# Where a matmul's operands begin: split activations and weights laid 16 bytes further apart

## The chip, the cores and the metric

The kernel runs on one core of one Trainium2 chip. The metric is the device time of one launch in microseconds (us), the median of several runs; less is better.

## The reference

One decoder block on x of 1 x 1024 x 1024 float32: a half-step SwiGLU FFN, a mixer, a second half-step FFN, and a final norm. Each part is preceded by an RMS norm, which is shifted, scaled and gated by vectors made from c.

```python
def swiglu(h, w1, w3, w2):
    return (jax.nn.silu(h @ w1) * (h @ w3)) @ w2
...
        h = modulate(rmsnorm(x, g_ffn1[l]), sh1, sc1)
        x = x + 0.5 * gt1[:, None, :] * swiglu(h, ffn1_w1[l], ffn1_w3[l], ffn1_w2[l])
        h = modulate(rmsnorm(x, g_mix[l]), sh2, sc2)
        x = x + gt2[:, None, :] * hybrid_mixer(
            h, w_in[l], lambda_q1[l], lambda_k1[l], lambda_q2[l], lambda_k2[l],
            subln_g[l], conv_w[l], conv_norm_g[l], w_out[l], cos, sin, lambda_init)
        h = modulate(rmsnorm(x, g_ffn2[l]), sh3, sc3)
        x = x + 0.5 * gt3[:, None, :] * swiglu(h, ffn2_w1[l], ffn2_w3[l], ffn2_w2[l])
```

The FFNs have D_MODEL 1024 and D_FF 2816. The mixer has 4 heads of differential attention and a short gated convolution.

## The kernel before

Activations lie transposed, 128 features by 512 positions to a tile; `X` holds the residual stream. All wide products are made from float32r parts: an operand a is split in hi and lo, and a product a b is three matmuls, hi hi, hi lo and lo hi, each 128 x 128 weights over a moving operand of 128 x 512. ACT writes the hi part (a copy to float32r) and DVE the lo part (a subtraction).

In an FFN the up part (`up`, `ph` 0 and 1 for the two FFNs) uses Strassen's scheme over 2 x 2 halves: seven products, `j` = 0 to 6. For product `j` the moving operand is `Bh[j]`, `Bl[j]`, four tiles of 128 x 512 each. A first group (`plain_group`) makes plain products with `Bh` and `Bl` of 0, 5, "B12" and 3. Then each `u` from 2 to 21 makes the seven jobs in the order of `j`. One job is 12 matmuls: four blocks k, and for each the three

```python
mm_open(PS[:, bank, :], Wh[:, t % SLOTS, w], Bh[j][:, k, :], fresh and k == 0, False)
mm_open(PS[:, bank, :], Wh[:, t % SLOTS, w], Bl[j][:, k, :], False, False)
made = mm_open(PS[:, bank, :], Wl[:, t % SLOTS, w], Bh[j][:, k, :], False, last and k == KH - 1)
```

The second argument is the weights, the third the moving operand; `t` counts jobs, so that job `t` finds its weights in slot `t % 8` of the ring `Wh`, `Wl`. The down part (`down`, `down_tile`) uses the same scheme with jobs `m`; here both operands come through the ring: the weights `Wh[:, 4 + m % 4, ...]` and `Wl` of the same slot, the moving operand `Wh[:, m % 4, :]` and `Wl` of that slot. `prep_hi`, `down_hi` (ACT) and `prep_lo`, `down_lo` (DVE) fill the ring. Every matmul is preceded by its own load of weights (engine PEld in the profile).

The mixer's projections have moving operands `Hh`, `Hl` and weights `Mh`, `Ml`; the projection to V has them the other way round; the last heads' output projection moves `Gh`, `Gl` or `G2` over `Wo`.

All tiles are placed by hand, with `place(..., like=address)`, in bytes from the start of a partition. `base` is 16512, K is 1024. The order on each engine is written out by hand; semaphores tie the engines together.

Of the kernel before, what the change touches and what calls it, by code (L numbers as in the profile page):

```python
# [6 lines left out]
F32R = mybir.dt.float32r  # L7
# [4 lines left out]
P = 128  # L12
# [3 lines left out]
KH = KT // 2  # L16
HALF = 512
# [55 lines left out]

PAIRS = 2 * NG
SLOTS = 8
AHEAD = 5
AHEAD_B = 3
N_UP = 8 + 7 * (PAIRS - 2)
# [72 lines left out]
def program(nc, up_w, down_w, units, ada, x_t, cols_d, lam_d, rope_d, square_d, out_t):  # L151
    ctx = ExitStack()
    with ctx:
# [3 lines left out]
        def place(name, shape, dtype=F32, like=None):  # L157

            size = 4
            for n in shape[1:]:  # L160
                size *= n
            offset = at[0] if like is None else like
            if like is None:
                at[0] += (size + 31) // 32 * 32
            return nc.alloc_sbuf_tensor_at(name, shape, dtype, offset=offset), offset

        K = 1024
        base = at[0]
        x_at = base + 88 * K + 64
        slot_at, raw_at, t_at, z_at, tmp_at = (x_at + n * K for n in (32, 64, 80, 96, 108))  # L170
        at[0] = tmp_at + 8 * K

        X, _ = place("X", [P, NH, KT, HALF], like=x_at)
# [3 lines left out]
        Bh, Bl = {}, {}  # L177
        for _j, _h, _l in ((0, base, base + 8 * K), (1, base + 16 * K, base + 24 * K), (2, base + 32 * K, base + 40 * K),
                           (3, base + 48 * K, base + 56 * K), (5, base + 64 * K, base + 72 * K),
                           (4, x_at + 24 * K, x_at + 16 * K), (6, x_at + 8 * K, x_at),  # L180
                           ("B12", z_at + 4 * K, tmp_at)):
            Bh[_j], _ = place(f"Bh{_j}", [P, KH, HALF], F32R, like=_h)
            Bl[_j], _ = place(f"Bl{_j}", [P, KH, HALF], F32R, like=_l)
        Sums, _ = place("Sums", [P, 4, HALF], like=base + 80 * K)
        Wh, _ = place("Wh", [P, SLOTS, HALF], F32R, like=slot_at)
        Wl, _ = place("Wl", [P, SLOTS, HALF], F32R, like=slot_at + 16 * K)
        Raw, _ = place("Raw", [P, 4, 2, HALF], like=raw_at)
        T, _ = place("T", [P, 8, HALF], like=t_at)
        Ada, _ = place("Ada", [P, 2, D], like=z_at)
        AdaSum, _ = place("AdaSum", [P, D], like=z_at + 8 * K)  # L190
        W2s, _ = place("W2s", [P, 4, HALF], like=tmp_at)
# [3 lines left out]
        RawB, _ = place("RawB", [P, 8, HALF], like=raw_at)  # L195

        AdaFirst, _ = place("AdaFirst", [P, KT, D], like=base)
        AdaSecond, _ = place("AdaSecond", [P, KT, D], like=base + 32 * K)
        AdaSum0, _ = place("AdaSum0", [P, D], like=t_at)
        AdaRow, _ = place("AdaRow", [P, D], like=t_at + 4 * K)  # L200
        Lam4, _ = place("Lam4", [P, 4, DH], like=t_at + 8 * K)
        LamP, _ = place("LamP", [P, 2, DH], like=t_at + 9 * K)


        Mh, _ = place("Mh", [P, RING, S], F32R, like=base)
        qk_at = base + 12 * K
        QK, _ = place("QK", [P, 2, S + 8], like=qk_at)
        CU, _ = place("CU", [P, S + 2], like=qk_at)
        CT, _ = place("CT", [P, S], like=qk_at + 4 * (S + 8))
        o_at = qk_at + 8 * (S + 8)  # L210
        O, _ = place("O", [P, QB, P], like=o_at)
        Mr, _ = place("Mr", [P, RING, S], like=o_at + 4 * K)
        h0_at = o_at + 16 * K
# [3 lines left out]
        Ml, _ = place("Ml", [P, RING, S], F32R, like=h0_at + 32 * K)  # L217

        Wo, _ = place("Wo", [P, 2, 2, S], F32R, like=h0_at)
        Rope, _ = place("Rope", [P, 2, S], like=h0_at + 44 * K)  # L220
        assert h0_at + 52 * K == x_at
        V, _ = place("V", [P, QB, HEADS * P], like=raw_at)
        Gh, _ = place("Gh", [P, GF, S], F32R, like=t_at)
        Gl, _ = place("Gl", [P, GF, S], F32R, like=t_at + 8 * K)
        NextQ, _ = place("NextQ", [P, S], like=t_at + 4 * K)
        NextK, _ = place("NextK", [P, S], like=t_at + 12 * K)

        G2, _ = place("G2", [P, 2, S + 8], F32R, like=qk_at)
        PR, _ = place("PR", [P, 3, S], like=z_at)
        SqSum, _ = place("SqSum", [P, NH, HALF], like=z_at)  # L230
        Sq, _ = place("Sq", [P, 2, HALF], like=z_at + 4 * K)
        Spread, _ = place("Spread", [P, NH, HALF], like=z_at + 8 * K)
        TmpA, _ = place("TmpA", [P, 2, HALF], like=tmp_at)
        TmpG, _ = place("TmpG", [P, 2, HALF], like=tmp_at + 4 * K)
        DT, _ = place("DT", [P, S], like=tmp_at + 4 * K)
        Out, _ = place("Out", [P, NH, KT, HALF], like=h0_at)

        Square, _ = place("Square", [P, 2, P])
        Cols, _ = place("Cols", [P, NCOLS])
        Mod, _ = place("Mod", [P, SECTIONS * KT])  # L240
        Scale, _ = place("Scale", [P, 4, KT])
        Gate, _ = place("Gate", [P, 3, KT])
        CAct, _ = place("CAct", [P, KT])
        Ones, _ = place("Ones", [P, 1])
        Mean, _ = place("Mean", [P, 1])
        MeanG, _ = place("MeanG", [P, 2])
        EpsC, _ = place("EpsC", [P, 2])
        Root, _ = place("Root", [P, 8])
        Inv, _ = place("Inv", [P, 8])
        LamS, _ = place("LamS", [P, 8])  # L250
        SubG, _ = place("SubG", [P, 1])
        NMax, _ = place("NMax", [P, 2])
        Sum, _ = place("Sum", [P, 2])
        RSum, _ = place("RSum", [P, QB, 2])
        Ratio, _ = place("Ratio", [P, 1])
        Junk, _ = place("Junk", [P, P])
        SqO, _ = place("SqO", [P, QB])
# [17 lines left out]
        def blk(b):  # L275
            return slice(b * P, (b + 1) * P)
# [123 lines left out]
        def _(sp):  # L400
# [11 lines left out]
            def spill(ph, g, q):  # L412
                sp.wait_ge(mul_done, silu_no(ph, g, q))
                sp.dma_start(g_dram[ph][g, q], T[:, 4 + q, :]).then_inc(spilled[q], 16)
# [25 lines left out]
            def block_of(ph):  # L440
# [4 lines left out]
                for t in range(8, N_UP):  # L445
                    u, j = 2 + (t - 8) // 7, (t - 8) % 7
                    u2, j2 = 2 + (t - 8 + AHEAD) // 7, (t - 8 + AHEAD) % 7
                    if j2 == 6 and u2 + 2 < PAIRS:
                        load_up(ph, u2 + 2)
                    up, jp = 2 + (t - 9) // 7, (t - 9) % 7  # L450
                    if t > 8 and up % 2 and jp >= 3:
                        spill(ph, up // 2, Q_OF_J[jp])
                    if t == N_UP - AHEAD:
                        for m in range(8):
# [145 lines left out]
        def _(act):  # L600
            def prep_hi(ph, o):

                slot = o % SLOTS
                if o < 8:
# [8 lines left out]
                else:  # L613
# [3 lines left out]
                    else:  # L617
                        act.wait_ge(prod, N_FFN * ph + max(o - SLOTS + 1, 8))
                    if j in (0, 5, 6):
# [61 lines left out]
            def t_hi(ph, n, j):  # L681
                h, k = {1: (0, 0), 2: (0, 0), 4: (1, 0), 6: (0, 0)}[j]
                for a in (0, 2):
                    act.wait_ge(t_sum, 8 * ph + 2 * n + a // 2 + 1)
                    nc.scalar.activation(Bh[j][:, a:a + 2, :], X[:, h, k + a:k + a + 2, :], ACT.Copy).then_inc(bt_hi, 1)

            def up(ph):
# [22 lines left out]
                for t in range(8, N_UP):  # L710
                    if t == 10:
                        t_hi(ph, 3, 6)
                    if t + AHEAD < N_UP:
                        prep_hi(ph, t + AHEAD)
                    elif t + AHEAD_B >= N_UP:
# [278 lines left out]
        def _(dve):  # L994
            def prep_lo(ph, o):

                slot = o % SLOTS
                if o < 8:
# [110 lines left out]
            def t_lo(ph, n, j):  # L1109
                h, k = {1: (0, 0), 2: (0, 0), 4: (1, 0), 6: (0, 0)}[j]  # L1110
                for a in (0, 2):
                    dve.wait_ge(bt_hi, 8 * ph + 2 * n + a // 2 + 1)
                    nc.vector.tensor_tensor(Bl[j][:, a:a + 2, :], X[:, h, k + a:k + a + 2, :],
                                            Bh[j][:, a:a + 2, :].bitcast(F32), ALU.subtract).then_inc(b_lo, 1)

            def up(ph):
# [37 lines left out]
                for t in range(8, N_UP):  # L1154
                    if t == 10:
                        t_add(ph, 3, 6)
                        t_lo(ph, 3, 6)
                    if t + AHEAD < N_UP:
                        prep_lo(ph, t + AHEAD)
                    elif t + AHEAD_B >= N_UP:  # L1160
# [369 lines left out]
        def _(pe):  # L1530
# [3 lines left out]
            def mm_open(out, lhs, rhs, first, last):  # L1534

                return nc.tensor.matmul(out, lhs, rhs, start=first, stop=last, skip_group_check=True)  # L1536
# [69 lines left out]
            def up(ph):  # L1606
                plain_group(ph)
                for t in range(8, N_UP):
# [8 lines left out]
                    for k in range(KH):  # L1617
                        w = blk(k)
                        mm_open(PS[:, bank, :], Wh[:, t % SLOTS, w], Bh[j][:, k, :], fresh and k == 0, False)
                        mm_open(PS[:, bank, :], Wh[:, t % SLOTS, w], Bl[j][:, k, :], False, False)  # L1620
# [450 lines left out]
```

## Time and profile before

| | |
|---|---|
| median of 3 runs | 1904.79 us (1899.98 to 1904.81) |
| span of the profiled execution | 1904.1 us |
| TensorE busy | 1834.6 us, 96% |
| DVE busy | 1262.7 us, 66% |
| ACT busy | 773.6 us, 41% |
| POOL busy | 269.8 us, 14% |

The profile gives one execution's span, from its first to its last instruction; the median of the runs is 0.7 us longer. Busy time of TensorE is counted from start to modelled end of matmuls that overlap, so how fast it gets through them is read from the starts.

### The profile page before, as it was taken

How to read it: one execution, taken by the hardware profiler on the slowest of the kernel's cores; microseconds unless marked ns; L12 is line 12 of the kernel's file. 1: busy time of each engine (PE TensorE's matmuls, PEld its weight loads, DVE VectorE, ACT ScalarE, POOL GpSimd, SP SyncE). 2: the span in 40 equal slices, each digit the busy share in tenths (PEclk: the TensorE clock that was granted, in tenths of full speed). 3: DMA queues.
4: the chain of work that ended last, by engine and by line, in shares of the span. 5: the costliest groups of instructions: out<-in, count | busy, mean ns of one | idle time of the engine just before them, and what ended most of it. 6: DMA issues, size and time to landing. Idle time of an engine off the chain costs nothing.

```text
span 1904.1 us, 22925 instructions
## 1 busy us (share of the span) xinstructions
PE 1834.6 (96%) x8248; PEld 1466.7 (77%) x8248; DVE 1262.7 (66%) x1952; ACT 773.6 (41%) x1392; POOL 269.8 (14%) x411
## 2 busy tenths in 40 slices
PE   5999999999999999999999999899999999999997
PEld 2878888888788877888876666687888888878885
DVE  5887777767486776444326668787667666577767
ACT  5643333333344555111125555563333333344445
POOL 2011211211210000000303330101111211112000
PEclk9999999999999999999999999999999999999998
DMA  8165565664775321111211110325454544477432
GB/s 316 64 230 198 198 218 192 225 210 168 265 216 155 95 64 74 45 45 45 67 33 45 45 34 1 140 83 197 160 189 170 204 156 168 158 261 217 128 99 89
DMA packets 100528, 269.76 MB, mean 142 GB/s; under 512 B 13120, under 2 KB 13504, under 8 KB 100288
## 3 DMA queue, kind: packets, MB, share of 16 engines
q1 hardware_dynamic: 62608, 146.30, 22.6%
q0 software_dynamic: 34304, 117.46, 18.2%
q10 hardware_dynamic: 3504, 4.53, 1.0%
q8 instruction: 66, 1.08, 0.2%
q14 instruction: 46, 0.38, 0.1%
HBM read 209.53 MB, written 54.53 MB: 139 GB/s over the span
## 4 chain that ended last, share of the span: by engine, by line
PE 84%; DVE 8%; ACT 4%; issue 2%; DMA 1%; ACTq 1%; POOL 1%; DVEq 0%; POOLq 0%
PE PS L1536 60%; PE PS L1532 24%; DMA AdaFirst<-ada 1%; PE PS L1956 1%; ACTq L877 1%; DVE X L1107 1%; DVE NMax L1447 1%; DVE Wl L1006 1%; DVE Ml L1246 0%; ACT X L676 0%; DVE SqSum L1312 0%; DVE TmpA L1330 0%; DVE X L1343 0%; DVE Wl L1041 0%; ACT PR L899 0%
## 5 line engine op out<-in xcount | busy, mean ns | idle before, releaser
L1536 PE MATMUL PS<-Bh,Wh 128*128 128x512 f32 x1120 | 441.4, 394 | 3.7 <-ACT T L659 3.7
L1536 PE MATMUL PS<-Bl,Wh 128*128 128x512 f32 x1120 | 440.6, 393 | 0.0
L1536 PE MATMUL PS<-Bh,Wl 128*128 128x512 f32 x1120 | 439.9, 393 | 0.0
L1536 PEld LDWEIGHTS PS<-Bh,Wh 128*128 128x128 f32 x1120 | 209.8, 187 | 55.7 <-issue 3.7
L1536 PEld LDWEIGHTS PS<-Bh,Wl 128*128 128x128 f32 x1120 | 209.8, 187 | 49.9
L1536 PEld LDWEIGHTS PS<-Bl,Wh 128*128 128x128 f32 x1120 | 209.8, 187 | 49.1
L1536 PE MATMUL PS<-Wh 128*128 128x512 f32 x616 | 240.3, 390 | 3.4 <-DVE Wl L1041 1.7
L1536 PE MATMUL PS<-Wh,Wl 128*128 128x512 f32 x616 | 239.7, 389 | 0.0
L1536 PE MATMUL PS<-Wl,Wh 128*128 128x512 f32 x616 | 239.7, 389 | 0.0
L1038 DVE TENSOR_TENSOR Wl<-RawB,Wh 128x512 fp32r<-128x512 f32 x154 | 106.6, 692 | 136.5 <-ACT Wh L634 135.3
L634 ACT ACTIVATE Wh<-RawB 128x512 fp32r<-128x512 f32 x154 | 97.3, 632 | 230.0 <-PE PS L1536 230.0
L659 ACT ACTIVATE T<-PS 128x512 f32<-128x512 f32 x120 | 71.7, 597 | 257.3 <-PE PS L1536 257.3
L1006 DVE TENSOR_TENSOR Wl<-Sums,Wh 128x512 fp32r<-128x512 f32 x160 | 110.3, 689 | 88.2 <-ACT Wh L624 88.1
L1536 PEld LDWEIGHTS PS<-Wh 128*128 128x128 f32 x616 | 115.6, 188 | 28.6 <-DVE T L1072 2.5
L1006 DVE TENSOR_TENSOR Wl<-Raw,Wh 128x512 fp32r<-128x512 f32 x136 | 94.6, 700 | 61.9 <-ACT Wh L624 61.4
L1536 PEld LDWEIGHTS PS<-Wl,Wh 128*128 128x128 f32 x616 | 115.7, 188 | 23.9
L1536 PEld LDWEIGHTS PS<-Wh,Wl 128*128 128x128 f32 x616 | 115.6, 188 | 23.9
L1532 PE MATMUL PS<-Hh,Mh 128*128 128x512 f32 x320 | 131.6, 411 | 2.1 <-DVE Hl L1336 1.3
L624 ACT ACTIVATE Wh<-Sums 128x512 fp32r<-128x512 f32 x160 | 98.4, 623 | 80.1 <-DVE Sums L1024 52.6
L1532 PE MATMUL PS<-Hl,Mh 128*128 128x512 f32 x320 | 127.4, 398 | 0.0
L1532 PE MATMUL PS<-Hh,Ml 128*128 128x512 f32 x320 | 126.8, 396 | 0.0
L1062 DVE TENSOR_TENSOR T<-T,PS 128x512 f32<-128x512 f32 x120 | 82.3, 686 | 47.2 <-PE PS L1536 45.2
(193 smaller groups left out, 2869.7 us busy)
## 6 DMA issues: line engine op xcount, KB each, us to landing
Raw<-up_w SPq DMA_DIRECT2D x86, 512.0 KB, 5.5
Ada<-ada POOLq DMA_DIRECT2D x72, 512.0 KB, 4.2
g_dram<-T SPq DMA_DIRECT2D x88, 256.0 KB, 2.1
W2s<-down_w POOLq DMA_DIRECT2D x88, 256.0 KB, 4.4
s_dram<-W2s POOLq DMA_DIRECT2D x88, 256.0 KB, 2.6
GQ<-g_dram POOLq DMA_DIRECT2D x88, 256.0 KB, 3.3
RawB<-s_dram SPq DMA_DIRECT2D x88, 256.0 KB, 2.8
RawB<-down_w SPq DMA_DIRECT2D x66, 256.0 KB, 2.7
```

What stands on the lines that cost most here:

```text
L624: nc.scalar.activation(Wh[:, slot, :], src, ACT.Copy).then_inc(w_hi, 1)
L634: nc.scalar.activation(Wh[:, 4 + m % 4, :], RawB[:, m % 8, :], ACT.Copy).then_inc(w_hi, 1)
L659: nc.scalar.activation(T[:, 4 * w + q, :], PS[:, x + (j == 1), :], ACT.Copy).then_inc(acopy, 1)
L877: act.dma_start(to[a:a + 32, :], TmpA[a ^ 32:(a ^ 32) + 32, slot, :]).then_inc(shifted[j % 2], 16)
L1006: nc.vector.tensor_tensor(Wl[:, slot, :], src, Wh[:, slot, :].bitcast(F32), ALU.subtract).then_inc(w_lo, 1)
L1038: nc.vector.tensor_tensor(Wl[:, 4 + m % 4, :], RawB[:, m % 8, :], Wh[:, 4 + m % 4, :].bitcast(F32), ALU.subtract).then_inc(w_lo, 1)
L1062: nc.vector.tensor_tensor(T[:, 4 * w + q, :], T[:, 4 * w + q, :], PS[:, x + (j != 4), :], ALU.add)\
L1107: nc.vector.tensor_tensor(out, left, right, ALU.subtract).then_inc(t_sum, 1)
L1447: nc.vector.tensor_reduce(NMax[:, c:c + 1], scores(c, 0, i + 1), AX.X, ALU.max, negate=True)\
L1532: return nc.tensor.matmul(out, lhs, rhs, start=first, stop=last)
L1536: return nc.tensor.matmul(out, lhs, rhs, start=first, stop=last, skip_group_check=True)
L1956: made = nc.tensor.transpose(PS[:, 4 + r, blk(b % 4)], PR[:, 2, blk(b)], ident)
```

## The change

Three kinds of addresses are moved; nothing else is touched. Each of the eight slots of `Wh` and `Wl` becomes 16 bytes wider, so that slot n begins 16 n bytes later than it did. The tiles `Bh[j]`, `Bl[j]` of `j` = 0, 1, 2, 3, 5 are moved up by 0, 32, 64, 96, 128 bytes, and of each `Bl` another 16. What lies behind them is moved up to make room, by multiples of 128 bytes but for `Sums` (160). The instructions of each engine, their order and their waits are the same as before.

```diff
@@ -73,6 +73,7 @@
 
 PAIRS = 2 * NG
 SLOTS = 8
+SKEW = 16
 AHEAD = 5
 AHEAD_B = 3
 N_UP = 8 + 7 * (PAIRS - 2)
@@ -166,8 +167,9 @@
 
         K = 1024
         base = at[0]
-        x_at = base + 88 * K + 64
-        slot_at, raw_at, t_at, z_at, tmp_at = (x_at + n * K for n in (32, 64, 80, 96, 108))
+        x_at = base + 88 * K + 192
+        slot_at = x_at + 32 * K
+        raw_at, t_at, z_at, tmp_at = (slot_at + n * K + 2 * SLOTS * SKEW for n in (32, 48, 64, 76))
         at[0] = tmp_at + 8 * K
 
         X, _ = place("X", [P, NH, KT, HALF], like=x_at)
@@ -179,11 +181,16 @@
                            (3, base + 48 * K, base + 56 * K), (5, base + 64 * K, base + 72 * K),
                            (4, x_at + 24 * K, x_at + 16 * K), (6, x_at + 8 * K, x_at),
                            ("B12", z_at + 4 * K, tmp_at)):
-            Bh[_j], _ = place(f"Bh{_j}", [P, KH, HALF], F32R, like=_h)
-            Bl[_j], _ = place(f"Bl{_j}", [P, KH, HALF], F32R, like=_l)
-        Sums, _ = place("Sums", [P, 4, HALF], like=base + 80 * K)
-        Wh, _ = place("Wh", [P, SLOTS, HALF], F32R, like=slot_at)
-        Wl, _ = place("Wl", [P, SLOTS, HALF], F32R, like=slot_at + 16 * K)
+            n = (0, 1, 2, 3, 5).index(_j) * 2 * SKEW if _j in (0, 1, 2, 3, 5) else 0
+            lead = SKEW // 4 if _j in (0, 1, 2, 3, 5) else 0
+            Bh[_j], _ = place(f"Bh{_j}", [P, KH, HALF], F32R, like=_h + n)
+            whole, _ = place(f"Bl{_j}", [P, lead + KH * HALF], F32R, like=_l + n)
+            Bl[_j] = whole[:, lead:lead + KH * HALF].rearrange("p (k s) -> p k s", k=KH)
+        Sums, _ = place("Sums", [P, 4, HALF], like=base + 80 * K + 10 * SKEW)
+        wide = HALF + SKEW // 4
+        Wh, _ = place("Wh", [P, SLOTS, wide], F32R, like=slot_at)
+        Wl, _ = place("Wl", [P, SLOTS, wide], F32R, like=slot_at + 16 * K + SLOTS * SKEW)
+        Wh, Wl = Wh[:, :, 0:HALF], Wl[:, :, 0:HALF]
         Raw, _ = place("Raw", [P, 4, 2, HALF], like=raw_at)
         T, _ = place("T", [P, 8, HALF], like=t_at)
         Ada, _ = place("Ada", [P, 2, D], like=z_at)
@@ -218,7 +225,7 @@
 
         Wo, _ = place("Wo", [P, 2, 2, S], F32R, like=h0_at)
         Rope, _ = place("Rope", [P, 2, S], like=h0_at + 44 * K)
-        assert h0_at + 52 * K == x_at
+        assert h0_at + 52 * K <= x_at
         V, _ = place("V", [P, QB, HEADS * P], like=raw_at)
         Gh, _ = place("Gh", [P, GF, S], F32R, like=t_at)
         Gl, _ = place("Gl", [P, GF, S], F32R, like=t_at + 8 * K)
```

## Rows read from the trace of the kernel before

**Rows 1.** The page: span; busy us of each engine, share, instructions.

```profile
span 1904.1 us, 22925 instructions
...
PE 1834.6 (96%) x8248; PEld 1466.7 (77%) x8248; DVE 1262.7 (66%) x1952; ACT 773.6 (41%) x1392; POOL 269.8 (14%) x411
```

**Rows 2.** The page: the chain of work that ended last, by engine and by line.

```profile
PE 84%; DVE 8%; ACT 4%; issue 2%; DMA 1%; ACTq 1%; POOL 1%; DVEq 0%; POOLq 0%
PE PS L1536 60%; PE PS L1532 24%; DMA AdaFirst<-ada 1%; PE PS L1956 1%; ACTq L877 1%; DVE X L1107 1%; DVE NMax L1447 1%; DVE Wl L1006 1%; DVE Ml L1246 0%; ACT X L676 0%; DVE SqSum L1312 0%; DVE TmpA L1330 0%; DVE X L1343 0%; DVE Wl L1041 0%
```

**Rows 3.** TensorE's groups by shape: count, busy us, mean ns, idle before; one per kind.

```profile
L1536 PE MATMUL PS<-Bh,Wh 128*128 128x512 f32 x1120 | 441.4, 394 | 3.7 <-ACT T L659 3.7
...
L1536 PE MATMUL PS<-Wh 128*128 128x512 f32 x616 | 240.3, 390 | 3.4 <-DVE Wl L1041 1.7 <-DVE T L1072 1.6
...
L1532 PE MATMUL PS<-Bh,Wh 128*128 128x512 f32 x96 | 40.3, 419 | 5.8 <-DVE Bl L1097 5.8
...
L1532 PE MATMUL PS<-BlB,Wh 128*128 128x512 f32 x32 | 12.5, 390 | 0.0
```

**Rows 4.** Windows, engine busy us (instructions): unit of seven jobs, jobs, down, mixer.

```profile
core 0: us, PE busy (x) PEld busy (x) DVE busy (x) ACT busy (x) POOL busy (x), PEclk, DMA share, GB/s
247.05:266.51 19.46, 19.46 (x85) 15.68 (x84) 16.85 (x24) 5.14 (x9) 4.83 (x9) 1.00 0.66 232
263.71:266.51 2.80, 2.80 (x13) 2.24 (x12) 1.14 (x2) 1.12 (x2) 2.14 (x4) 1.00 0.91 345
266.51:269.25 2.74, 2.74 (x13) 2.25 (x12) 1.92 (x3) 1.15 (x2) 0.54 (x1) 1.00 0.91 286
269.25:272.05 2.80, 2.80 (x13) 2.25 (x12) 2.63 (x4) 1.15 (x2) 0.42 (x1) 1.00 0.23 83
503.16:519.48 16.32, 16.32 (x73) 13.52 (x72) 8.93 (x14) 6.92 (x12) 3.23 (x6) 1.00 1.02 376
827.49:835.73 8.24, 8.24 (x37) 6.76 (x36) 2.68 (x4) 0.00 (x0) 0.00 (x0) 1.00 0.00 1
836.42:839.17 2.75, 2.75 (x14) 2.25 (x12) 0.69 (x1) 0.64 (x1) 0.00 (x0) 1.00 0.00 0
952.44:958.07 5.63, 5.63 (x25) 4.51 (x24) 0.00 (x0) 0.00 (x0) 0.00 (x0) 1.00 0.26 93
1199.49:1202.29 2.80, 2.80 (x13) 2.25 (x12) 0.81 (x2) 1.89 (x4) 0.00 (x0) 1.00 0.84 275
```

**Rows 5.** Timeline of TensorE: start us, us; the job of `j` = 4.

```profile
266.51 0.39 PE L1536 MATMUL PS<-Bh,Wh 128*128 128x512 f32 x1
266.74 0.40 PE L1536 MATMUL PS<-Bl,Wh 128*128 128x512 f32 x1
266.98 0.39 PE L1536 MATMUL PS<-Bh,Wl 128*128 128x512 f32 x1
267.20 0.40 PE L1536 MATMUL PS<-Bh,Wh 128*128 128x512 f32 x1
267.44 0.39 PE L1536 MATMUL PS<-Bl,Wh 128*128 128x512 f32 x1
267.67 0.39 PE L1536 MATMUL PS<-Bh,Wl 128*128 128x512 f32 x1
267.89 0.39 PE L1536 MATMUL PS<-Bh,Wh 128*128 128x512 f32 x1
268.12 0.39 PE L1536 MATMUL PS<-Bl,Wh 128*128 128x512 f32 x1
```

**Rows 6.** DVE's subtractions on line 1006, by input.

```profile
L1006 DVE TENSOR_TENSOR Wl<-Sums,Wh 128x512 fp32r<-128x512 f32 x160 | 110.3, 689 | 88.2 <-ACT Wh L624 88.1
...
L1006 DVE TENSOR_TENSOR Wl<-Raw,Wh 128x512 fp32r<-128x512 f32 x136 | 94.6, 700 | 61.9 <-ACT Wh L624 61.4
```

## The prediction

> **What bounds the kernel now.** I read the page first: TensorE is busy for 96% of the span, DVE for 66%, ACT for 41% [rows 1], and the chain of work that ended last lies on TensorE for 84%, 60% of the span on line 1536 alone [rows 2]. Line 1536 issues the products of both FFNs; as long as they follow each other without a gap, each nanosecond more or less between two of them is one in the result. So I read next how many there are, by tile, and then, in windows that begin and end on a job of the program, how far apart two of them start. Their durations (390 to 419 ns, [rows 3]) are of no use for that, since matmuls overlap; the distance from start to start (the pitch) is.
>
> The pitch is not one number [rows 4]. In the windows the count of weight loads is the count of matmuls, and TensorE is busy throughout. A job of `j` = 3 (from 263.71) takes 2.80 us for 12 matmuls, 233.3 ns each; the job of `j` = 4 behind it 2.74 us, 228.3 ns; that of `j` = 5 again 2.80 us. In the down part (from 503.16) 72 matmuls take 16.32 us, 226.7 ns. The granted clock is 1.00 in all. DMA doesn't make the difference: the two 2.80 us jobs have a DMA share of 0.91 and 0.23. The slots of the weights are the same in both.
>
> What differs is where the operands begin. I call an address modulo 128 its phase: `base` is 16512, so phase 0, and `x_at` and all behind it phase 64. Before the change `Wh` and `Wl` have phase 64, `Bh` and `Bl` of `j` = 0, 1, 2, 3, 5 phase 0, those of 4, 6 and "B12" phase 64. Call the moving operand's phase less the weights' the distance. Distance 64 (opposite) goes with 233.3 ns, distance 0 with 226.7. The start of the job of `j` = 4 shows how the fast pitch is reached [rows 5]: starts 0.23, 0.24, 0.22, 0.24, 0.23, 0.22, 0.23 us apart. The change of distance takes six or seven matmuls to settle, which is why such a job stands at 228.3 and not at 226.7.
>
> Three further places tell more [rows 4]. In the projections (from 827.49, 36 matmuls in 8.24 us, 228.9 ns) the moving operand always has phase 64, the weights 0, 0, 64 in turn. In the values' projection (from 952.44, 24 in 5.63 us, 234.5 ns) the weights keep 64 and the moving operand goes 0, 0, 64. In the output projection of the last heads (from 1199.49, 12 in 2.80 us, 233.3 ns) the weights keep 64 and the moving operand goes 0, 32, 0. So the weights' phase counts too, not the moving operand's alone; and distance 96 (32 less 64) is as dear as distance 64.
>
> **The change, part by part.** No instruction, wait or transfer is added, removed or moved; only addresses change. After it, slot n of `Wh` and of `Wl` has phase 64 + 16n; `Bh` of `j` = 0, 1, 2, 3, 5 has 0, 32, 64, 96, 0 and `Bl` 16 more; `j` = 4, 6 and "B12" keep 64. `X`, the DMAs' targets and everything of the mixer keep their phases (`Sums` goes to 32).
>
> ACT writes and DVE reads and writes at new phases. I cost that at nothing: the same subtraction takes 689 ns with an input at phase 0 and 700 ns with all at 64 [rows 6]. What hides it otherwise is TensorE's own 19.46 us in a unit of seven jobs, in which DVE is busy for 16.85 and ACT for 5.14 [rows 4]; DVE's 24 instructions there would each have to grow by 0.1 us before anything waits.
>
> *The down part.* A job `m` reads its weights in slot 4 + m % 4 and its moving operand in slot m % 4. Before, both have phase 64: distance 0. After, they are 64 apart for every m: distance 64 throughout. The matmuls there are three groups of 616, 1848 [rows 3]. Bounds: no loss, 0; the pitch of the other rows at constant distance 64, 233.3 - 226.7 = 6.67 ns, x 1848 = 12.3 us. Between them lies the projections' row, with moving 64 over weights 0 in two of three: (228.9 - 226.7) x 1848 = 4.1 us. I take 12.3, since there, as in the up jobs of `j` = 3, the distance stays for the whole job and doesn't alternate.
>
> *The up part.* Seven jobs go round eight slots, so each `j` meets all eight distances about equally often. Matmuls on line 1536: 3 x 1120 = 3360, of which 5/7 = 2400 at distance 64 now and 960 at distance 0; the plain group adds 3 x 96 = 288 at 64 and 3 x 32 = 96 at 0 [rows 3]. So 2688 stand at 233.3, 960 at 228.3, 96 at 226.7. What a distance costs is known for 0 (228.3 with the settling), 64 and 96 (233.3 each); five are not shown. Bounds for these: 228.3 and 233.3. I take the middle, 230.8: of the five, 16 and 112 lie beside the cheap 0, 48 and 80 beside the dear 64, and 32 between. Mean: (228.3 + 2 x 233.3 + 5 x 230.8) / 8 = 231.1 ns. The shift of 16 between `Bh` and `Bl` I cost at nothing: the row with 0, 32, 0 stands at 233.3, as without the alternation.
> - 2688 x (231.1 - 233.3) = -5.9 us
> - 960 x (231.1 - 228.3) = +2.7 us
> - 96 x (231.1 - 226.7) = +0.4 us
>
> With the five unknown at 228.3 the mean is 229.6 and the three terms are -9.9 + 1.2 + 0.3 = -8.4 us; at 233.3 it is 232.7, and they are -1.6 + 4.2 + 0.6 = +3.2 us.
>
> Sum: -5.9 + 2.7 + 0.4 + 12.3 = +9.5 us on the profiled execution's span of 1904.1 us, 1913.6. The median of the three runs is 1904.8, 0.7 above that span, so 1914.3.
>
> A rule speaks against any effect. The rows just read show two pitches, 233.3 and 226.7 ns, at the same clock. The Trainium skill, "TensorE: Matmul & The Clock Gate" (Part 2, Step-by-step), has it that TensorE reads moving operand and weights through two independent ports, so that loading the next weights takes no read bandwidth from the running matmul; by that the sum is 0. "SBUF — State Buffer" (Who interferes with whom) says likewise that TensorE waits for no one. The trace doesn't agree: its pitch follows the pair of phases.
>
> **The rivals.**
> - *Gain and loss cancel.* The five unknown distances are all cheap (228.3): -8.4 + 12.3 = +3.9 us, 1908.7, inside what can't be told from no change. For it speaks that the change of distance settles in six matmuls; against it that 96 is dear.
> - *Faster.* The opposite distance is dear only with the weights ahead: moving 64 over weights 0 would be cheap. For it speaks the projections' 228.9. Then the down part loses nothing, and with cheap neighbours the sum is -8.4 us, 1896.4. It decides for faster once the down part loses under about 2.7 us, 1.5 ns a matmul. Its far end is every product at 226.7: 2688 x 6.67 + 960 x 1.67 = 19.5 us less, 1885.
> - *Dearer than either pitch.* Changing phases cost by themselves, as in the values' projection (234.5), and all products come there: 2688 x 1.2 + 960 x 6.2 + 96 x 7.8 + 1848 x 7.8 = 24.4 us, 1929. Against it: 0, 32, 0 costs nothing.
> - *No effect of phases.* The two pitches come from something else that goes with the tiles, such as how high in memory they lie (`Bh` of 4 and 6 lie behind `x_at`, the others ahead of it). Then 1904.8. Against it: the projections have the same pitch with `Hh0` ahead of `x_at` (228.9) and with `Hh1` behind it (12 in 2.75 us, 229) [rows 4].
>
> **How the numbers follow.** Forecast 0.45, cancelling 0.19, faster 0.22, dearer still 0.10, no effect 0.04. 0.3% (5.7 us) is about what a measurement of this kernel can tell from no change. Faster 0.22; same 0.19 + 0.04 = 0.23; slower 0.45 + 0.10 = 0.55. The forecast's own range is 1911 (down part at 12.3, up part at -6) to 1920 (12.3 + 3.2). For 8 in 10 it takes in the faster rival down to 1894 and goes up to 1922, leaving out most of "dearer still" and the far end of "faster".
>
> **What would show it.** The down part's windows: 233.3 instead of 226.7 ns between starts; if 226.7 stays there, the main term falls. The up jobs: pitches that differ by slot, 227 to 233, with a mean near 231, and the jobs of `j` = 4 and 6 no longer faster than the rest. Projections, values and attention: unchanged. DVE's and ACT's durations within 2% of before. Wrong would be the whole if a distance not shown before has a pitch under 226 or over 240.

## The result, and the profile after

The median of five runs is 1909.49 us, against 1903.05 before: the ratio is 1.0034, with a 95% interval of 1.0018 to 1.0051. The kernel became 6.4 us slower; the forecast was 9.5 slower. The time lies in the wide range of 1894 to 1922 us, and 1.5 us below the forecast's own range of 1911 to 1920. The profiled execution has a span of 1911.3 us, 7.2 above that of [rows 1].

The page after: the span, the engines and the chain. Against [rows 1, 2] TensorE is busy 8.8 us longer, DVE and ACT as long as before, and TensorE's share of the chain went from 84 to 86%.

```profile
span 1911.3 us, 22925 instructions
...
PE 1843.4 (96%) x8248; PEld 1468.7 (77%) x8248; DVE 1261.7 (66%) x1952; ACT 774.1 (41%) x1392; POOL 270.4 (14%) x411
...
PE 86%; DVE 7%; ACT 3%; issue 1%; DMA 1%; ACTq 1%; POOL 1%; DVEq 0%; POOLq 0%
```

Where the 7.2 us lie is read from windows over the stages. First those of the kernel before: up and down part of the first FFN, the mixer, up and down part of the second. The columns are as in [rows 4].

```profile
43.68:496.49 452.81, 449.46 (x1977) 363.85 (x1977) 336.72 (x483) 173.63 (x291) 78.86 (x147) 0.99 0.54 188
496.49:711.69 215.20, 212.17 (x942) 175.03 (x941) 153.66 (x247) 102.72 (x175) 17.74 (x33) 1.00 0.51 156
711.69:1230.17 518.48, 489.36 (x2353) 380.57 (x2351) 280.67 (x467) 194.32 (x419) 76.40 (x55) 0.98 0.16 52
1230.17:1674.00 443.83, 443.43 (x1937) 358.77 (x1937) 306.97 (x450) 174.81 (x294) 67.23 (x124) 1.00 0.47 164
1674.00:1889.68 215.68, 212.01 (x941) 174.87 (x940) 155.44 (x248) 101.46 (x174) 17.75 (x33) 1.00 0.51 158
```

The same stages after the change:

```profile
44.81:497.60 452.79, 449.52 (x1977) 365.00 (x1977) 336.69 (x483) 173.84 (x291) 78.88 (x147) 0.99 0.53 188
497.60:716.60 219.00, 216.49 (x941) 175.01 (x940) 153.73 (x246) 102.81 (x175) 17.73 (x33) 1.00 0.50 153
716.60:1234.39 517.79, 489.46 (x2353) 380.62 (x2351) 279.50 (x467) 194.25 (x419) 76.95 (x55) 0.98 0.16 52
1234.39:1678.29 443.90, 443.52 (x1936) 360.01 (x1937) 307.00 (x450) 175.14 (x294) 67.27 (x124) 1.00 0.47 165
1678.29:1897.96 219.67, 216.44 (x941) 174.90 (x940) 155.50 (x248) 101.41 (x174) 17.75 (x33) 1.00 0.50 155
```

Both up parts take as long as before (452.81 and 452.79 us, 443.83 and 443.90). The down parts take 3.80 and 3.99 us more. The mixer takes 0.7 less; what lies ahead of the first stage takes 1.1 more and what lies behind the last 1.1 less.

Windows after the change, which answer to [rows 4]: an up job of `j` = 4 and the one of `j` = 5; 12 jobs of the down part; the projections with `Hh0` and with `Hh1`; the values' projection; the last heads' output projection.

```profile
267.55:270.33 2.78, 2.78 (x13) 2.25 (x12) 1.95 (x3) 1.15 (x2) 0.54 (x1) 1.00 0.70 267
270.33:273.14 2.81, 2.81 (x14) 2.26 (x13) 2.60 (x4) 1.15 (x2) 0.43 (x1) 1.00 0.42 122
509.75:543.09 33.34, 33.34 (x146) 27.04 (x145) 24.00 (x38) 13.85 (x24) 6.45 (x12) 1.00 0.76 247
829.36:837.60 8.24, 8.24 (x37) 6.76 (x36) 2.68 (x4) 0.00 (x0) 0.00 (x0) 1.00 0.00 1
838.29:841.07 2.78, 2.78 (x13) 2.25 (x12) 0.69 (x1) 0.63 (x1) 0.00 (x0) 1.00 0.00 0
954.73:960.29 5.56, 5.56 (x25) 4.51 (x24) 0.00 (x0) 0.00 (x0) 0.00 (x0) 1.00 0.25 94
1202.71:1205.48 2.77, 2.77 (x13) 2.25 (x12) 0.78 (x2) 1.89 (x4) 0.00 (x0) 1.00 0.78 290
```

In the down part 144 matmuls take 33.34 us, 231.5 ns each, against 226.7. The up job of `j` = 4 takes 2.78 us (231.3) where it took 2.74, that of `j` = 5 2.81 for 12 (2.80 before). And the mixer did move, though modulo 128 none of its tiles had: with `Hh0` 36 matmuls still take 8.24 us, but with `Hh1` 12 take 2.78 instead of 2.75; the values' projection went from 5.63 to 5.56, the output projection from 2.80 to 2.77.

DVE's subtractions, which answer to [rows 6], are no dearer at the new phases:

```profile
L1013 DVE TENSOR_TENSOR Wl<-Sums,Wh 128x512 fp32r<-128x512 f32 x160 | 110.3, 689 | 87.3 <-ACT Wh L631 87.2
...
L1013 DVE TENSOR_TENSOR Wl<-Raw,Wh 128x512 fp32r<-128x512 f32 x136 | 93.9, 695 | 63.4 <-ACT Wh L631 63.3
```

### The profile page after: what moved, and what is told of

Read it like the earlier page. It is cut to its first block, busy times and chain, and to the rows that moved or that the text cites. A ratio compares the mean times of both kernels' runs of the same rounds, so it can differ in the third digit from the quotient of the medians.

```text
span 1911.3 us, 22925 instructions
## 1 busy us (share of the span) xinstructions
PE 1843.4 (96%) x8248; PEld 1468.7 (77%) x8248; DVE 1261.7 (66%) x1952; ACT 774.1 (41%) x1392; POOL 270.4 (14%) x411
## 4 chain that ended last, share of the span: by engine, by line
PE 86%; DVE 7%; ACT 3%; issue 1%; DMA 1%; ACTq 1%; POOL 1%; DVEq 0%; POOLq 0%
PE PS L1543 60%; PE PS L1539 25%; PE PS L1963 1%; DMA AdaFirst<-ada 1%; ACTq L884 1%; DVE NMax L1454 1%; DVE Ml L1253 1%; DVE SqSum L1319 0%; DVE TmpA L1337 0%; DVE Wl L1048 0%; ACT PR L906 0%; DVE Wl L1013 0%; DMA TmpA<-TmpA 0%; DVE CT L1419 0%; DVE Wl L1045 0%
```

## The experiments

Throughout, the distance is the moving operand's address less the weights'. Three runs were timed several times (`same64`, `mixer_too`, `odd16`); the others have one time each and are told by their traces. The diffs are shortened: remarks in brackets are not code, and lines that only make room for the moved tiles are left out.

### One phase for all operands of the FFNs: same64

```diff
-            Bh[_j], _ = place(f"Bh{_j}", [P, KH, HALF], F32R, like=_h)
-            Bl[_j], _ = place(f"Bl{_j}", [P, KH, HALF], F32R, like=_l)
+            n = {0: 64, 1: 64, 2: 64, 3: 64, 5: 64}.get(_j, 0)
+            (both placed at like=_h + n, like=_l + n)
-        Sums, _ = place("Sums", [P, 4, HALF], like=base + 80 * K)
+        Sums, _ = place("Sums", [P, 4, HALF], like=base + 80 * K + 64)
```

> The kernel before with the five low pairs of Bh and Bl moved up by 64 bytes, so that every FFN operand begins at 64 modulo 128: distance 0 everywhere. If the pitch follows the distance between moving operand and weights (theory of the prediction), all seven kinds of up job stand at 226.7 ns and the run is 2688 x 6.67 + 960 x 1.67 = 19.5 us faster, about 1884 us. If it followed something else that goes with the tiles (how high in memory they lie, their order), the five stay at 233.3 ns and the time at 1903 us.

Measured: 1886.27 us, ratio to the kernel before 0.9911 (0.9895 to 0.9928). Its stages, up, down, mixer, up:

```profile
44.55:489.10 444.55, 441.93 (x1976) 365.31 (x1977) 336.39 (x483) 173.61 (x291) 79.19 (x147) 0.99 0.55 192
489.10:704.23 215.13, 212.07 (x941) 175.03 (x940) 153.62 (x247) 102.83 (x175) 17.79 (x33) 1.00 0.50 156
704.23:1223.80 519.57, 490.41 (x2354) 381.08 (x2352) 279.76 (x467) 194.84 (x419) 77.13 (x55) 0.98 0.16 52
1223.80:1659.23 435.43, 434.11 (x1936) 359.52 (x1937) 306.99 (x450) 174.64 (x294) 67.48 (x124) 1.00 0.47 168
```

The up parts lose 8.26 and 8.40 us, the down part none; that is 16.7 of the 19.5 expected. Of the 2.8 us that are missing, 1.9 lie where two starts are over 300 ns apart: beyond a usual pitch such places hold 0.9 us more than before in the first up part and 1.0 in the second, nearly all in `u` = 2, the first unit of seven jobs. In the second this is idle time (443.83 - 443.43 = 0.40 us before, 435.43 - 434.11 = 1.32 now). In the first, idle time fell by 0.7, but behind a wait of 2.33 us for ACT the granted clock was 0.55 from 101.07 to 104.84 us (the lower level, 1.2 GHz, for most of it), and matmuls started 427 ns apart. The median job of each `j` stands at 226.7 ns from its first matmul on; where the distance doesn't change there is nothing to settle. The tiles moved by 64 bytes and kept their order and height in memory, so height is not what sets the pitch. Whether an operand's own place modulo 256 counts beside the distance is asked of `moved96` and `odd16` below.

### The distances one by one: near, far, wide

```diff
-        x_at = base + 88 * K + 64
+        x_at = base + 88 * K + 64 + 512
...
+            n = {0: 16, 1: 32, 2: 48, 3: 64, 5: 80}.get(_j, 0)      (near)
+            n = {0: 96, 1: 112, 2: 128, 3: 160, 5: 192}.get(_j, 0)  (far)
+            n = {0: 224, 1: 256, 2: 288, 3: 320, 5: 448}.get(_j, 0) (wide)
```

> The kernel before with Bh and Bl of j = 0, 1, 2, 3, 5 moved up by 16, 32, 48, 64, 80 bytes (all behind them by 512): constant distances of -48, -32, -16, 0, 16 bytes between moving operand and weights, the down part as before. By the theory of the prediction, with distances modulo 128, the second half of the jobs stands at 233.3 ns for j = 1 (96), 226.7 for j = 3 (0), and between them for j = 0, 2 and 5, nearer to 226.7 for j = 2 and 5. A rival, in which only equal phases are cheap: 233.3 for all but j = 3. Whole time between 1888 and 1900 us.

> As the run before it, with shifts of 96, 112, 128, 160, 192 bytes: distances 32, 48, 64, 96, 128. Modulo 128 (theory of the prediction): 233.3 ns for j = 2 (64) and j = 3 (96), 226.7 for j = 5 (128 is 0). Rival: the period is 256 or more, since the projections whose moving operand Hh1 went up by 128 bytes had another pitch after the change (231 against 228.9 ns): then j = 5 is not at 226.7, and j = 2 (64) and j = 3 (96) need not stand where -64 and -32 stand.

> As the two runs before it, with shifts of 224, 256, 288, 320, 448 bytes: distances 160, 192, 224, 256, 384. Modulo 128: j = 0 as 32, j = 1 as 64 (233.3 ns), j = 2 as 96 (233.3), j = 3 and j = 5 at 226.7. Modulo 256: j = 1 as -64 (233.3), j = 2 as -32, j = 3 (256) at 226.7, j = 5 as 128. With a period of 512 or more, j = 3 isn't at 226.7.

Measured: 1896.7, 1900.63 and 1896.5 us. Windows of one job (12 matmuls) each. Run near, `j` = 0, 2, 5, distances -48, -16, 16:

```profile
254.12:256.94 2.82, 2.82 (x14) 2.26 (x12) 2.82 (x5) 0.00 (x0) 0.53 (x1) 1.00 0.31 113
259.74:262.46 2.72, 2.72 (x13) 2.25 (x12) 2.41 (x5) 1.12 (x2) 0.53 (x1) 1.00 0.94 361
267.94:270.72 2.78, 2.78 (x13) 2.26 (x12) 2.63 (x4) 1.16 (x2) 0.40 (x1) 1.00 0.39 112
```

Run far, `j` = 0, 2, 5, distances 32, 64, 128:

```profile
254.92:257.72 2.80, 2.80 (x13) 2.25 (x12) 2.80 (x5) 0.00 (x0) 0.54 (x1) 1.00 0.37 117
260.48:263.24 2.76, 2.76 (x13) 2.25 (x12) 2.49 (x5) 1.12 (x2) 0.53 (x1) 1.00 1.03 355
268.80:271.60 2.80, 2.80 (x14) 2.25 (x13) 2.61 (x4) 1.16 (x2) 0.42 (x1) 1.00 0.29 92
```

Run wide, `j` = 1 and 3, distances 192 and 256:

```profile
258.56:261.35 2.79, 2.79 (x14) 2.25 (x12) 2.66 (x5) 1.12 (x2) 0.55 (x1) 1.00 0.85 302
264.14:266.86 2.72, 2.72 (x13) 2.25 (x12) 1.14 (x2) 1.12 (x2) 2.14 (x4) 1.00 0.93 336
```

A whole job still holds the settling from the job ahead of it. Without that (from a job's seventh matmul to the start of the next job, over 6; median of the 40 jobs of a kind in each trace) the pitches are:

| distance | -64 | -48 | -32 | -16 | 0 | 16 | 32 | 48 | 64 | 96 | 128 | 160 | 192 | 224 | 256 |
|---|---|---|---|---|---|---|---|---|---|---|---|---|---|---|---|
| ns | 233.3 | 234.8 | 233.3 | 226.7 | 226.7 | 231.3 | 233.5 | 230.0 | 228.8 | 233.3 | 233.3 | 233.8 | 233.3 | 233.3 | 226.7 |

(-64 from the kernel before, 0 from same64. In the run near the job at 0, `j` = 3, stands at 228.3 by the same measure: it comes behind a job at -16 and is settled only from its ninth matmul on, at 227.) All weights here begin at 192 modulo 256, and at the distances of ±16 and ±48 the moving operand begins at an odd multiple of 16. The prediction's modulus of 128 falls: 64 stands at 228.8 where -64 stands at 233.3, and 128 at 233.3 where 0 stands at 226.7. Modulo 256 it holds: 192 is as -64, 224 as -32, 256 as 0. Cheap are 0 and -16 alone. In the mean over the twelve distances the pitch is 231.6 ns; the up parts of the changed kernel, whose distances go round, have 232.0 from start to start. Its down part has 231.5, but there the distances don't go round, so that the mean doesn't explain it.

### Each part of the change alone: slots_only, tiles_only

```diff
-            n = (0, 1, 2, 3, 5).index(_j) * 2 * SKEW if _j in (0, 1, 2, 3, 5) else 0
-            lead = SKEW // 4 if _j in (0, 1, 2, 3, 5) else 0
+            n = 0                        (slots_only)
+            lead = 0
...
-        wide = HALF + SKEW // 4
+        wide = HALF                      (tiles_only; Wl at slot_at + 16 * K)
```

> The changed kernel with the activations' tiles back at their old phases: only the eight slots of Wh and Wl are 16 bytes further apart. By the distances, up jobs at a mean of 231 to 233 ns and the down part as in the changed kernel (231.5): about 1908 us, the whole loss. If the tiles' own shifts were what costs, 1903 us or less.

> The changed kernel with the eight slots back at 2048 bytes apart: only the activations' tiles are moved (and what lies behind them by 128). The down part is back at 226.7 ns. Up jobs at distances modulo 256 of 64, 96, 128, 160, 192 for j = 0, 1, 2, 3, 5: 229 for j = 0 and 233 to 234 for the others, j = 4 and 6 near 228. Time 1900 to 1903 us.

Measured: 1910.2 and 1905.09 us. Run slots_only, first up and down part and second up part:

```profile
44.80:496.42 451.62, 448.45 (x1976) 364.13 (x1977) 336.74 (x483) 173.86 (x291) 78.89 (x147) 1.00 0.53 189
496.42:715.43 219.01, 216.46 (x941) 175.06 (x940) 153.82 (x246) 102.84 (x175) 17.73 (x33) 1.00 0.48 153
1231.62:1675.53 443.91, 443.70 (x1937) 360.10 (x1937) 306.96 (x450) 175.03 (x294) 67.23 (x124) 1.00 0.46 165
```

Run tiles_only, the same:

```profile
45.13:497.10 451.97, 448.53 (x1976) 364.49 (x1977) 336.75 (x483) 173.90 (x291) 78.92 (x147) 0.99 0.54 189
497.10:712.31 215.21, 212.16 (x942) 174.98 (x940) 153.67 (x247) 102.74 (x175) 17.73 (x33) 1.00 0.49 156
1232.26:1673.81 441.55, 441.01 (x1937) 358.42 (x1937) 306.91 (x450) 175.02 (x294) 67.27 (x124) 1.00 0.46 165
```

The slots alone have the down part's whole loss (219.01 us against 215.20) and leave the up parts 1.1 us shorter together. The tiles alone leave the down part where it was and take 3.1 us from the up parts (893.5 against 896.6). The changed kernel has the down part's loss and, of the up parts' gain, nothing.

The time of tiles_only missed its expectation of 1900 to 1903 us: its mixer is 1.5 us longer than before and its first stage begins 1.4 later, which takes back most of the gain. Its pitches missed too. Settled, `j` = 0, 1, 2, 3, 5 stand at 232.8, 234.5, 231.2, 231.2 and 231.5 ns, where the table has 228.8, 233.3, 233.3, 233.8 and 233.3 for the distances of `Bh`. Two things differ from the table's runs: `Bl` begins 16 bytes further than `Bh`, so that the distance changes within the job, and the weights begin at 64 modulo 256. Job by job the two together cost or give up to 4 ns; in the mean of the five (232.2 against 232.5) they are next to nothing.

### The down part's term by itself: down_m64, down_p64

```diff
+        class Halves:                    (slots 0 to 3 and 4 to 7 as two tiles)
+            def __init__(self, name, at):
+                self.parts = [place(f"{name}{n}", [P, SLOTS // 2, HALF], F32R, like=at + n * 8 * K + by)[0]
+                              for n, by in ((0, 0), (1, 64))]      (down_p64: (0, 64), (1, 256))
...
+        Wh, Wl = Halves("Wh", slot_at), Halves("Wl", slot_at + 16 * K + 256)
```

Both start from same64.

> The run same64 with slots 4 to 7 of Wh and Wl 64 bytes up: in the down part the moving operand stands at a constant distance of -64 from the weights. The prediction's term of the down part by itself: 233.3 ns instead of 226.7, 12.3 us. The up jobs whose weights lie in slots 4 to 7 stand at -64 too, half of 3744 matmuls, 12.5 us. Together 1886 + 24.8 = 1911 us. If the down part is dear for another reason than the distance, it stays at 226.7 and the time at 1899.

> The run same64 with slots 0 to 3 of Wh and Wl 64 bytes up and slots 4 to 7 256 up: in the down part a constant distance of +64, where the run down_m64 had -64. With the pitches of the up jobs at +64 (228.8 ns in the run far) the down part is 3 to 4 us dearer than in same64, not 12; the up jobs with weights in slots 0 to 3 stand at -64, 12.5 us. About 1902 us. If the sign doesn't matter (period 128), the down part stands at 233.3 and the time at 1911.

Measured: 1910.05 and 1904.7 us. Run down_m64, the first down part and 12 jobs of it:

```profile
495.06:715.61 220.55, 218.16 (x941) 175.19 (x940) 153.81 (x247) 102.97 (x175) 17.79 (x33) 1.00 0.48 152
507.37:540.97 33.60, 33.60 (x145) 27.07 (x144) 24.00 (x38) 13.86 (x24) 6.47 (x12) 1.00 0.75 244
```

Run down_p64, the same:

```profile
493.36:710.22 216.86, 214.15 (x942) 175.10 (x941) 153.71 (x246) 102.76 (x175) 17.79 (x33) 1.00 0.49 154
505.44:538.40 32.96, 32.96 (x146) 27.05 (x145) 24.00 (x38) 13.85 (x24) 6.47 (x12) 1.00 0.78 258
```

At a constant -64 the 144 matmuls take 33.60 us, 233.3 ns each, and the first down part is 5.42 us longer than in same64; twice that is 10.8 us of the term of 12.3. TensorE's busy time there grew by 6.09 us, twice that is 12.2; the difference is that less is waited. At +64 they take 32.96 us, 228.9 each, and the part is 1.73 longer. So the sign counts, and a constant distance of -64 costs what the prediction put on it.

### The phase without the distance: moved96, pairs256, odd16

Moved96 starts from same64, with `at = [16512 + 96]`. Pairs256 starts from the changed kernel, odd16 from same64:

```diff
-        Wl, _ = place("Wl", [P, SLOTS, wide], F32R, like=slot_at + 16 * K + SLOTS * SKEW)      (pairs256)
+        Wl, _ = place("Wl", [P, SLOTS, wide], F32R, like=slot_at + 16 * K + 2 * SLOTS * SKEW)
...
+            n = {0: 80, 1: 80, 2: 80, 3: 80, 5: 80}.get(_j, 0)                                 (odd16)
+        Wh, Wl = (place(name, [P, 4 + SLOTS * HALF], F32R, like=at)[0][:, 4:].rearrange("p (n s) -> p n s", n=SLOTS)
+                  for name, at in (("Wh", slot_at), ("Wl", slot_at + 16 * K + 256)))
```

> The run same64 with every tile of the kernel 96 bytes further up: all distances as in same64, all absolute phases others. If only the distance counts, 226.7 ns in all FFN jobs and 1886 us. If the phase itself counts, other pitches in all of them.

> The changed kernel with Wl 128 bytes further up, a multiple of 256 behind Wh slot by slot, so that the distances modulo 256 no longer alternate between -64 and +64 within a job of the down part. The down part goes from 231.5 to the 233.3 ns of a constant -64, 3 to 4 us more, about 1913 us in all. If the 231.5 has another cause (the shift by 16 from job to job), it stays.

> The run same64 with Wh, Wl and the five low pairs of Bh and Bl 16 bytes further up: distance 0 in the down part and in the up jobs of j = 0, 1, 2, 3, 5, as in same64, but all operands now begin at an odd multiple of 16 (80); j = 4 and 6 stand at -16. In the run pairs256 the down jobs at a constant -64 took 229 to 230 ns where the operands begin at odd multiples of 16 and 232.5 to 233 where at even ones, so the phase itself counts for something there. If 226.7 is the least there is, all FFN jobs stay there and the time is that of same64, 1886 us. If an odd multiple of 16 is cheaper by itself at every distance, the pitch falls below 226.7, by up to 4 ns, and the time by up to 20 us.

Moved96: 1887.47 us; first up and down part as in same64, which shows for distance 0, and for it alone, that moving both operands by 96 bytes changes nothing:

```profile
44.58:489.26 444.68, 441.91 (x1977) 365.30 (x1977) 336.52 (x483) 173.50 (x291) 78.90 (x147) 0.99 0.55 192
489.26:704.46 215.20, 212.14 (x942) 174.98 (x940) 153.66 (x247) 102.75 (x175) 17.74 (x33) 1.00 0.51 156
```

Pairs256: 1912.45 us. Its down part didn't go to 233.3 ns. Two jobs in a row, 12 matmuls each, whose moving operands begin at 64 and at 80 modulo 128:

```profile
509.66:512.45 2.79, 2.79 (x13) 2.26 (x12) 1.29 (x2) 1.15 (x2) 0.54 (x1) 1.00 1.05 387
512.45:515.21 2.76, 2.76 (x13) 2.25 (x12) 1.29 (x2) 1.16 (x2) 0.54 (x1) 1.00 1.03 384
```

Both have the constant distance -64. The first, whose operands begin at multiples of 32, takes 2.79 us (232.8 ns by the start times); the second, at odd multiples of 16, 2.76 (229.7). The next two jobs, at 96 and 112, stand at 232.6 and 229.3. The expectation falls: the first down part takes 218.67 us, 0.3 less than in the changed kernel and not 2 more, so that the time, which was expected at about 1913, agrees for another reason. At a constant -64 it is the jobs at odd multiples of 16 that keep the mean at 231.1 ns.

The changed kernel has nearly the same mean, 231.5, by another pattern. Its jobs alternate between -64, +64 and +64, since `Wl` lies 128 bytes from `Wh` modulo 256. By slot (0 to 3) they stand at 233.3, 231.1, 231.3 and 230.4 ns; here those of slots 0 and 2, at 64 and 96 modulo 128:

```profile
509.75:512.55 2.80, 2.80 (x14) 2.25 (x13) 1.29 (x2) 1.15 (x2) 0.54 (x1) 1.00 1.05 381
515.32:518.09 2.77, 2.77 (x13) 2.25 (x12) 1.90 (x3) 1.16 (x2) 0.54 (x1) 1.00 1.04 386
```

Slot 2 begins at a multiple of 32 and is cheaper by 2 ns all the same, which a constant -64 doesn't show (232.6). So neither odd multiples of 16 alone nor the distances alone (by the table 230.3 for each job) give its 231.5.

Odd16: 1908.63 us, ratio to the kernel before 1.0015 (0.9997 to 1.0033). First down part, and 12 jobs of it:

```profile
492.82:710.64 217.82, 215.28 (x941) 174.73 (x940) 153.78 (x246) 102.93 (x175) 17.77 (x33) 1.00 0.50 154
504.92:538.04 33.12, 33.12 (x145) 26.98 (x144) 24.00 (x38) 13.87 (x24) 6.46 (x12) 1.00 0.80 254
```

Both expectations fall. At distance 0, but with both operands at an odd multiple of 16, the 144 matmuls take 33.12 us, 230.0 ns, 3.3 more than in same64. The up jobs at distance 0 stand at 230.0 in the first FFN too. In the second, at the same addresses, most stand at 233.3 and some at 230.0. Two jobs of `j` = 1 with weights in the same slot, in the units `u` = 10 and 18 of the second FFN:

```profile
1443.24:1446.00 2.76, 2.76 (x14) 2.25 (x12) 1.41 (x2) 1.12 (x2) 0.00 (x0) 1.00 0.97 349
1600.46:1603.26 2.80, 2.80 (x14) 2.26 (x13) 2.38 (x4) 1.12 (x2) 0.67 (x2) 1.00 0.91 285
```

(The run also moves the tiles from `Raw` on by 32 modulo 256, the mixer's `V`, `Gh`, `Gl` among them. Its mixer is 4.8 us longer than that of same64; the granted clock there is 0.97 against 0.98, so that this is not shown to come from the tiles.) Equal addresses modulo 256 gave 226.7 ns, once settled, where both operands begin at multiples of 32 (same64, moved96), and not here.

### The mixer's tiles too: mixer_too

From same64:

```diff
-        Mh, _ = place("Mh", [P, RING, S], F32R, like=base)
-        qk_at = base + 12 * K
-        QK, _ = place("QK", [P, 2, S + 8], like=qk_at)
+        Mh, _ = place("Mh", [P, RING, S], F32R, like=base + 64)
+        qk_at = base + 12 * K + 64
+        QK, _ = place("QK", [P, 2, S + 64], like=qk_at)      (CT, o_at, G2 with S + 64 too; x_at + 512)
```

> The run same64 with the mixer's tiles moved too, so that Mh, G2 and its second half also begin where Hh, Ml, Gh and Wo begin modulo 256. If the pitch follows the distance modulo 256, the projections (960 matmuls at 230.3 ns before) and the values' projection (192 at 234.4) go to 226.7: about 5 to 6 us less than same64, 1880 us. If the alternation there has another cause, 1886 us.

Measured: 1883.38 us, ratio to the kernel before 0.9896 (0.9876 to 0.9916), the best of all. The mixer, the projections (36 matmuls) and the values' projection (24):

```profile
703.16:1217.97 514.81, 486.55 (x2353) 381.30 (x2351) 279.87 (x467) 194.41 (x419) 76.09 (x55) 0.98 0.16 52
816.90:825.06 8.16, 8.16 (x37) 6.76 (x36) 2.68 (x4) 0.00 (x0) 0.00 (x0) 1.00 0.00 1
940.51:945.95 5.44, 5.44 (x26) 4.51 (x24) 0.00 (x0) 0.00 (x0) 0.00 (x0) 1.00 0.28 96
```

In these windows both projections stand at 226.7 ns (8.16 us for 36, 5.44 for 24). In the first no DMA is at work (0.00), in the second neither DVE nor ACT nor POOL, so that no other engine explains both. The mixer is 3.7 us shorter than before and 4.8 shorter than in same64, where 5 to 6 were expected: in the mean over all projections with `Hh` and `Hl` the pitch is 228.3, from 230.2. The interval overlaps that of same64, so that this step's gain is read from the trace and not from the times.

## Why the prediction was right or wrong

- **The number**: +7.2 us on the spans against +9.5, and partly by luck. The down part came 4.5 us under its term and the up part 2.8 above its own, two misses that cancel in part; the mixer's -0.7 was not in the sum. The rival *cancelling*, at 1908.7 us, lies nearer to the 1909.49 than the forecast's 1914.3, but its mechanism (-8.4 us in the up part) is not what happened.
- **That the pitch depends on how the operands lie to each other, at the same clock**: right; same64 turns it into a gain of 16.7 us in the up parts. The rule of "TensorE: Matmul & The Clock Gate" in the Trainium skill (Part 2, Step-by-step), by which loading the next weights takes no read bandwidth from the running matmul, would leave the pitch alone. The traces don't agree: with nothing but addresses changed, the same matmuls stand 226.7 to 234.8 ns apart.
- **The down part's term, +12.3 us**: right in sign and right that it costs, too large. It was +7.8. A constant -64 does cost 6.67 ns a matmul (down_m64), but the step "the distance stays for the whole job and doesn't alternate" failed: modulo 256 two of a job's three matmuls stand at +64. Besides, odd multiples of 16 have prices of their own (pairs256: 229.3 and 229.7 ns at a constant -64). Measured are 4.8 ns a matmul in place of 6.67, 8.9 us; how much of the difference is due to which is not separated. About 1 us less is waited, too: TensorE's idle time in the two down parts went from 3.03 and 3.67 to 2.51 and 3.23 us.
- **The up part's three terms, -2.8 us together**: 0.0. The mean was 231.1 by the prediction and is 232.0. Jobs of `j` = 0, 1, 2, 3, 5 went from 233.3 to 232.0 ns, -3.2 us in 2400 matmuls where -5.3 was costed; those of 4 and 6 from 228.5 to 232.1, +3.4 us where it was +2.7; the plain group didn't gain. The five unknown distances were put halfway between bounds of 228.3 and 233.3, which don't hold: measured are 226.7 to 234.8, and of twelve distances modulo 256 only 0 and -16 are cheap. The shift by 16 within a job, costed at nothing, was not separated from the rest; in tiles_only the five jobs that have it stand where the table puts them in the mean, and not job by job.
- **"Phase" as an address modulo 128**: wrong, it is 256. In the up part it cost little, since the counts per distance are even in either case. In the down part it hid the alternation. And "projections, values and attention: unchanged" failed with it: `Hh1`, `V`, `Gh` and `Gl` went up by an odd multiple of 128.
- **DVE and ACT at nothing**: right, 689 and 695 ns for DVE's subtractions against 689 and 700 [rows 6], and both engines are as long busy as before.
- **Settling**: right that a change of distance costs some matmuls; same64 shows its absence. Six or seven is not the most: `j` = 4 in the run far, behind a job at 96, takes nine.
- **The other rivals**: the faster one's premise, that +64 is cheap, proved true (228.8), but one matmul in three stays at -64. "No effect" and "dearer than either pitch" are ruled out by the down part's 231.5 and the up part's 232.0.

Open is what makes the period of 256 and the difference between even and odd multiples of 16; the runs show it, and don't tell the cause. How the other distances of the table stand where both operands begin elsewhere was not measured one by one.

## What to carry to other kernels

Where matmuls follow each other without a gap, read the distance from start to start by tile, not their durations; two levels at one clock are a reason to look at the addresses. Put weights and moving operand of float32r products at the same address modulo 256, and at multiples of 32: here that was worth 1% with no instruction changed. Spreading addresses evenly bought about the mean of all distances (232.0 ns), not the best (226.7).

## What the hardware showed that was not expected

The pitch is no function of the two addresses alone. In the second FFN of odd16 the jobs at distance 0 stand at 233.3 ns in the units `u` = 3 to 7, at 230.0 from 10 to 13 and at 233.3 again from 15 to 19, at the same addresses and at a granted clock of 1.00 in the two jobs shown. The last heads' output projection has the same addresses in `G2` and `Wo` before and after the change, and still 12 of its matmuls took 2.80 us before [rows 4] and 2.77 after. So the sequence seems to keep one of several rhythms; that it depends on how it was entered is a guess, and what switches it was not tested.

And it takes up to nine matmuls to settle after a change of distance, though each loads its own weights: in the run far, the job of `j` = 4 (distance 0, behind 96) has starts 229, 233, 236, 224, 231, 236, 228, 232 and 231 ns apart before it reaches 227.
